# Two-block network on one core: the two rotary embeddings get their swapped halves from transfers inside SBUF instead of from permutation products

## The reference

```python
def apply_partial_rope(t, cos, sin):        # block one, ROPE_DIM = 16
    half = ROPE_DIM // 2
    t1 = t[..., :half]
    t2 = t[..., half:ROPE_DIM]
    rot = jnp.concatenate([t1 * c - t2 * s, t2 * c + t1 * s], axis=-1)
    return jnp.concatenate([rot, t[..., ROPE_DIM:]], axis=-1)

def _rope(x, pos):                          # block two, d = 64
    half = d // 2
    x1, x2 = xf[..., :half], xf[..., half:]
    out = jnp.concatenate([x1 * cos - x2 * sin, x2 * cos + x1 * sin], axis=-1)
```

## Time and profile before

| | |
|---|---|
| median of 3 runs | 1817.74 us (1811.52 to 1818.07) |
| the profiled execution | 1816.34 us, of which the trace's span is 1814.5 us |
| PE busy | 1708.3 us, 94% |
| DVE busy | 1047.8 us, 58% |
| ACT busy | 737.9 us, 41% |
| POOL busy | 63.0 us, 3% |
| chain that ended last | PE 81%, DVE 11%, ACT 5% |
| mean granted TensorE clock | 0.976 |

### The profile page before, as it was taken

The page is one execution under the profiler, slowest core; times in us unless marked ns, Lnnn a source line. Parts: engine busy times, 40 slices in busy tenths (PEclk is TensorE's granted clock), DMA queues, the critical chain, the costliest instruction groups (busy, mean ns, idle before and its releaser), DMA issues.

```text
span 1814.5 us, 22668 instructions
## 1 busy us (share of the span) xinstructions
PE 1708.3 (94%) x7488; PEld 1324.0 (73%) x7488; DVE 1047.8 (58%) x2091; ACT 737.9 (41%) x1392; POOL 63.0 (3%) x43
## 2 busy tenths in 40 slices
PE   5999999999998997799899999998999899999999
PEld 3777667777876765337688888886888678888887
DVE  7787766666456698963655564366444543333334
ACT  4363766663343233783443322324223244332322
POOL 0020000000000063000000000000000000000000
PEclk9999999999998997999899999998999899999999
DMA  6342334433331121002255554252333232232333
GB/s 232 135 166 95 123 133 158 145 139 134 95 91 57 47 61 45 1 1 70 73 198 193 185 186 163 91 199 83 102 97 100 70 93 92 93 102 95 97 101 104
DMA packets 55812, 201.65 MB, mean 111 GB/s; under 512 B 6192, under 2 KB 6320, under 8 KB 55600
## 3 DMA queue, kind: packets, MB, share of 16 engines
q1 hardware_dynamic: 55728, 200.57, 33.1%
HBM read 198.44 MB, written 2.10 MB: 111 GB/s over the span
## 4 chain that ended last, share of the span: by engine, by line
PE 81%; DVE 11%; ACT 5%; issue 2%; POOL 0%; DMA 0%; DVEq 0%; ACTq 0%; POOLq 0%
PE bank L450 25%; PE bank L452 24%; PE bank L451 24%; PE bank L563 2%; DVE G L1390 1%; ACT SB L964 1%; DVE SB L1535 1%; PE bank L552 1%; DVE H_lo L1384 1%; DVE W_lo L1320 1%; ACT PT L978 1%; PE bank L533 1%; DVE SB L1892 1%; PE bank L660 1%; DVE WORK L1810 1%
## 5 line engine op out<-in xcount | busy, mean ns | idle before, releaser
L450 PE MATMUL bank<-H_hi,W_hi 128*128 128x512 f32 x1416 | 578.7, 409 | 22.0 <-DVE H_lo L1384 12.2
L451 PE MATMUL bank<-H_lo,W_hi 128*128 128x512 f32 x1416 | 556.8, 393 | 0.0
L452 PE MATMUL bank<-H_hi,W_lo 128*128 128x512 f32 x1416 | 556.5, 393 | 0.0
L1320 DVE TENSOR_TENSOR W_lo<-RAW,W_hi 128x512 fp32r<-128x512 f32 x538 | 351.4, 692 | 196.3 <-ACT W_hi L839 180.6
L839 ACT CAST W_hi<-RAW 128x512 fp32r<-128x512 f32 x538 | 313.0, 618 | 234.9 <-PE bank L452 211.6
L450 PEld LDWEIGHTS bank<-H_hi,W_hi 128*128 128x128 f32 x1416 | 268.1, 189 | 120.0 <-issue 44.3
L451 PEld LDWEIGHTS bank<-H_lo,W_hi 128*128 128x128 f32 x1416 | 269.2, 190 | 58.1 <-issue 7.0
L452 PEld LDWEIGHTS bank<-H_hi,W_lo 128*128 128x128 f32 x1416 | 268.7, 190 | 58.0
L450 PE MATMUL bank<-A_hi,W_hi 128*128 128x512 f32 x352 | 137.0, 389 | 0.0
L452 PE MATMUL bank<-A_hi,W_lo 128*128 128x512 f32 x352 | 136.9, 389 | 0.0
L451 PE MATMUL bank<-A_lo,W_hi 128*128 128x512 f32 x352 | 136.9, 389 | 0.0
(11 more groups left out here) (255 smaller groups left out, 1915.9 us busy)
## 6 DMA issues: line engine op xcount, KB each, us to landing
RAW<-weights SPq DMA_DIRECT2D x269, 512.0 KB, 3.6
AW<-ada SPq DMA_DIRECT2D x100, 512.0 KB, 3.6
X<-x_t SPq DMA_DIRECT2D x4, 512.0 KB, 5.6
y_t<-X SPq DMA_DIRECT2D x8, 256.0 KB, 2.0
LW<-lru_w SPq DMA_DIRECT2D x1, 1024.0 KB, 12.9
CROW<-crow SPq DMA_DIRECT2D x1, 512.0 KB, 10.9
ROPE<-rope SPq DMA_DIRECT2D x1, 512.0 KB, 13.7
CS<-constants SPq DMA_DIRECT2D x1, 386.5 KB, 8.1
```

Of the source, the lines that this page charges most:

```text
L450: pe.matmul(dst, wh, ch(hi, k), start=(k == 0), stop=False)
L451: pe.matmul(dst, wh, ch(lo, k), start=False, stop=False)
L452: mm = pe.matmul(dst, wl, ch(hi, k), start=False, stop=(k == chunks - 1))
L1320: dve.tensor_tensor(W_lo[:, w], RAW[:, c:c + HALF], W_hi[:, w], ALU.subtract).then_inc(lo_done, 1)
```

## The change

The 24 products with a permutation (10 with rot1, 14 with rot2) are removed from PE. In their place SP issues, per chunk, four DMA transfers from SBUF to SBUF (`swap_halves`): for each of the two heads the lower half's rows go to where the upper half's belong and the other way round. In block one each moves 8 partitions of 512 columns (16 KB), in block two 32 partitions (64 KB). They write QX1 (block one, two buffers in the place of Y2) or QX (block two, two buffers), and DVE's second product reads that in place of the PSUM bank. In block one the rows that do not turn are set to zero once, by POOL, at the start. DVE waits for half_in, one semaphore for each buffer, 64 for the four transfers.

```diff
@@ block.sync @@
+            def swap_halves(c, dst, src, half):
+                for head in (0, HD):
+                    for a, b in ((head, head + half), (head + half, head)):
+                        sp.dma_start(dst[a:a + half, :], src[b:b + half, :]).then_inc(half_in[c % 2], 16)
+
+            def swap1(c):
+                sp.wait_ge(qraw, c + 1)
+                if c == 0:
+                    sp.wait_ge(x1_zero, 1)
+                if c >= 2:
+                    sp.wait_ge(rope_done, c - 1)
+                swap_halves(c, ch(QX1, c % 2), ch(QR1, c % 2), 8)
+
+            def swap2(i):
+                sp.wait_ge(head_in, i + 1)
+                sp.wait_ge(rope_done, 10 + i - 1)
+                swap_halves(i, ch(QX, i % 2), ch(QN, i % 3), 32)
+
             for t in range(0, T_FFN0):
                 raw(Tile(t + 4))
+                if T_Q < t <= T_Q + 10:
+                    swap1(t - T_Q - 1)
+                if T_QKV2 + 1 < t <= T_QKV2 + 7:
+                    swap2(t - T_QKV2 - 2)
+                if T_QKV2 + 9 < t <= T_QKV2 + 17:
+                    swap2(t - T_QKV2 - 4)
                 if t in ADA_AT:
                     ada_load(ADA_AT[t] % 4, ADA_AT[t] + 4)
@@ block.tensor @@
-            def rot1(c):
-                pe.wait_ge(qraw, c + 1)
-                if c >= 2:
-                    pe.wait_ge(rope_done, c - 1)
-                pe.matmul(ps[5 + c % 2][:], cs("rot1"), ch(QR1, c % 2), start=True, stop=True).then_inc(rot_mm, 1)
-
             for c in range(1, 10):
-                linear(Tile(T_Q + c), H_hi, H_lo, between=lambda k: rot1(c - 1) if k == 3 else None)
-            values(Tile(T_V), between=lambda k: rot1(9) if k == 3 else None)
+                linear(Tile(T_Q + c), H_hi, H_lo)
+            values(Tile(T_V))
-            def rot2(i):
-                pe.wait_ge(head_in, i + 1)
-                pe.wait_ge(rope_done, 10 + i)
-                bank = 5 if i == 13 else 3
-                pe.matmul(ps[bank][:], cs("rot2"), ch(QN, i % 3), start=True, stop=True).then_inc(rot_mm, 1)
...
+            pe.wait_ge(rope_done, 10 + 10)
             qk(16, (0, 1))
             query_columns(7)
-            rot2(13)
-            pe.wait_ge(rope_done, 10 + 13)
             qk(16, (2, 3))
             qk(17, (0, 1, 2))
...
-            pe.wait_ge(rope_done, 10 + 14)
             for s in range(16, 32):
+                if s < 18:
+                    pe.wait_ge(rope_done, (10 + 12, 10 + 14)[s - 16])
@@ block.gpsimd @@
+            pool.memset(QX1[:, :], 0.0).then_inc(x1_zero, 1)
@@ block.vector @@
             def rope1_out(c):
-                dve.wait_ge(rot_mm, c + 1)
+                dve.wait_ge(half_in[c % 2], 64 * (c // 2 + 1))
...
-                link(dve.tensor_tensor(RAB1[:, S:2 * S], ps[5 + c % 2][:], ROPE[:, S:2 * S], ALU.mult))
+                link(dve.tensor_tensor(RAB1[:, S:2 * S], ch(QX1, c % 2), ROPE[:, S:2 * S], ALU.mult))
...
             def rope2_out(i):
-                dve.wait_ge(rot_mm, 10 + i + 1)
+                dve.wait_ge(half_in[i % 2], 64 * (5 + i // 2 + 1))
...
-                turned(i, ch(QN, i % 3) if i < 6 else None, ps[5 if i == 13 else 3][:], dst)
+                turned(i, ch(QN, i % 3) if i < 6 else None, ch(QX, i % 2), dst)
...
-            rope2_out(13)
             score(16, 2)
             score(16, 3)
             minus_max(16)
+            rope2_out(13)
             for h in range(3):
                 score(17, h)
```

More of the change, by code:

```diff
@@ L37 @@
 _at = 0
-for _name, _n in (("ident", P), ("rot1", P), ("rot2", P), ("centre", P), ("sel_all", 1), ("sel_head", 2),
+for _name, _n in (("ident", P), ("rot2", P), ("centre", P), ("sel_all", 1), ("sel_head", 2),
                   ("mask_prev", P), ("mask_diag", P), ("sin_sign", 1), ("inv_freq", 1)):
@@ L62, in constant_columns @@
     put("ident", np.eye(P))
[L63 to L68, removed]
+    rot = np.zeros((P, P), np.float32)
+    for head in (0, HD):
+        for i in range(HD):
+            rot[head + (i + HD // 2) % HD, head + i] = 1.0
+    put("rot2", rot)
     put("sel_all", np.full((P, 1), 1.0 / (KC * P)))
@@ L280, in build @@
         QN = at("QN", 3 * S, unit[4] + S * 12)
+        QX = at("QX", 2 * S, unit[4] + S * 24)
         RAB = at("RAB", 2 * S, unit[6])
@@ L288, in build @@
         G1 = at("G1", 2 * S)
+        y2 = cursor[0]
         Y2 = at("Y2", 2 * S)
+        QX1 = at("QX1", 2 * S, y2)
         qr1 = sb1
@@ L320, in build @@
         ta_done, iu_done, states_done = sem("ta_done"), sem("iu_done"), sem("states_done")
-        qraw, rot_mm, rope_done, v_done = sem("qraw"), sem("rot_mm"), sem("rope_done"), sem("v_done")
+        qraw, rope_done, v_done = sem("qraw"), sem("rope_done"), sem("v_done")
+        x1_zero, half_in = sem("x1_zero"), [sem("half_in0"), sem("half_in1")]
         head_in, head_sq = sem("head_in"), sem("head_sq")
@@ L698, in in_qi1 @@
                     head_columns(ch(SQ, 0), 0, 4).then_inc(kcol_mm, 1)
-                if k == 3:
-                    rot2(0)
             def in_qi2(k):
@@ L704, in in_qi2 @@
                     head_rows(0)
-                if k == 3:
-                    rot2(1)
             def in_qi3(k):
@@ L711, in in_qi3 @@
                     pe.matmul(ps[7][:], cs("rot2"), ch(QR, 1), start=True, stop=True).then_inc(ki_rot, 1)
[L712 to L717, removed]
             def in_k1(k):
@@ L723, in in_k1 @@
                     head_columns(ch(SQ, 0), 8, 4).then_inc(kcol_mm, 1)
-                if k == 3:
-                    rot2(4)
                 if k < 7:
@@ L735, in in_values @@
                     head_rows(1)
-                if k == 3:
-                    rot2(5)
                 index(2, k)
@@ L747, in body @@
                             query_columns(c - 1)
-                        if k == 3:
-                            rot2(6 + c - 1)
                 return body
@@ L761, in _ @@
             linear(Tile(T_QKV2), H_hi, H_lo, first=h_ready(1))
-            for c, body in enumerate((in_qi0, in_qi1, in_qi2, in_qi3, in_k0, in_k1)):
+            for c, body in enumerate((in_qi0, in_qi1, in_qi2, in_qi3, None, in_k1)):
                 linear(Tile(T_QKV2 + 1 + c), H_hi, H_lo, between=body)
```

## The result

The changed kernel takes 1839.97 us (median of 4, 1836.04 to 1842.36) where the kernel before takes 1816.74 (median of 4, 1811.52 to 1818.07). The ratio is 1.0127, 95% interval 1.0105 to 1.0149: less than 2%, but clear of no change. The profiled execution of after took 1839.14 us with a span of 1837.4. The forecast was 1832, range 1815 to 1843, slower at 75%. The direction and the mechanism of block one held; the loss is 23 us where 15.5 were forecast.

A forecast was written before the change was run, and what follows sets the result against it. The prediction took PE to set the pace before the change, and a loop through SP's queue after it in block one. Block one +19.4, clock +1, block two -4.9 gave +15.5 on 1816.3: 1832 us, range 1815 to 1843.

The forecast's parts named there:

- The loop: Block one, chunks 1 to 7: transfers queue behind a load awaiting DVE's reduction; period 9.4 us, values 19.4 us later.
- The landing of 5.1 us: Block one: the four transfers land behind load and weight tile, 5.1 us after the reduction, 1.3 us of it covered.
- the lower bound: Block one: small transfers need not wait for large ones, landing after 2.9 us; period 7.2 us, values 4 us later.
- the upper one: Block one: each issue costs SP 0.43 us and the last lands in 4.5; landing 7.1 us, period 11.4 us.
- PE sets the pace, a period of 6.35: Block one before the change: DVE's turns come 6.35 us apart, each after waiting 0.8 us for PE's product.
- Rival A: Whole kernel: PE is the bound and transfers are hidden; up to 21 us gained on rotations, about 1801 us; 6%.
- The clock: Block one: PE's clock dips after idling, hidden inside the loop, costing 1 us (0 to 2) at the values' start.
- Rival C: Block one's loop: PE's clock falls and stays low, seven tiles cost 1.5 us more each, 1842 us; 12%.
- The 19 us pass to the end: After block one's values: everything behind needs them, so the 19 us delay carries through to the kernel's end.
- Block two: Keys gain 4.4 us, sine products lose 1, the moved last turn gains 1.5: together -4.9 us (-1 to -12).
- I take 1 us in all (0 to 3): Block two: eight sine products reading SBUF instead of PSUM beside GpSimd, 0 to 0.38 us more each, 1 us together.
- Rival B: Small transfers pass the large ones, landing in 2.9 us; block one loses 4, block two gains 5, 1816 us; 18%.

The follow-up runs named there:

- the four kernels of the table above: The changed kernel (1839.97 us) and three edits of it: two transfers per chunk in block one (1837.03), modulation loads cut to 16 partitions (1836.39), both edits (1829.85).
- block1_only: Changed kernel with block two's products and the last turn's old place restored, so only block one's rotations go by transfers: 1842.07 us, ratio 1.0134.
- the small load: Changed kernel with the modulation loads of steps 8 to 15 cut from 128 partitions to 16, all waits and issues kept: 1836.39 us.

## Why the prediction was right, and where its sizes were off

**The loop** was as forecast: SP's order, the four transfers behind load and tile, seven waits of DVE for a DMA, turns 9.8 to 10.2 us apart up to chunk 6 (9 to 10 was the mark), PE idle inside. The waits are longer than the mark of 3 to 4 us: 4.3 to 4.6, and 6.0 for chunk 7. Reversing the order alone takes all of it away, 29 us against the changed kernel.

**The landing of 5.1 us** was the mis-sized term. The six waits of the loop ended 5.6 to 5.85 us after the reduction (139.93 - 134.36 = 5.57; 150.06 - 144.21 = 5.85), and chunk 7's 7.2 us (171.75 - 164.55). The sum took SP's four issues for hidden behind the landing of the tile; they take 2.67 us and end 3.6 us after the reduction, and the transfers need some 2 us more: 147.81 to 150.06 is 2.25 us, 137.94 to 139.93 is 1.99. The value "2.0 us" stood in the lower bound and "each issue costs SP like a tile's" in the upper one; the truth joins the two, with 0.66 us in place of 0.43. Chunk 7 is the one behind whose transfers a weight tile is issued at once, at 168.21 above; in each of the four kernels of the table above it waits 1.4 to 1.6 us longer than the chunk before (6.00 against 4.64 us in the changed kernel). What holds it was not tried.

In numbers, +25.8 against +19.4: 0.7 us was lost before the first period, six periods of 10.0 in place of 9.4 are 3.7 us, chunk 7's landing 2.1.

**"PE sets the pace, a period of 6.35"** was read from two turns, and it holds for the whole stretch, though the earlier turns look otherwise. Here are turns of DVE, and then PE's rotations, in the trace of before:

```profile
110.65 0.69 DVE L1462 TENSOR_TENSOR RAB<-QR,ROPE 128x512 f32<-128x512 f32 x1
...
116.06 0.69 DVE L1462 TENSOR_TENSOR RAB<-QR,ROPE 128x512 f32<-128x512 f32 x1
```

```profile
107.62 1.02 PE L517 MATMUL bank<-QR,CS 128*128 128x512 f32 x2
...
113.97 1.02 PE L517 MATMUL bank<-QR,CS 128*128 128x512 f32 x2
...
120.31 1.02 PE L517 MATMUL bank<-QR,CS 128*128 128x512 f32 x2
```

The turns from 105.17 to 121.45 are 5.4 to 5.5 us apart with no wait before them, but the rotations are 6.35 us apart, and PE is busy for all of the 17.00 us from 105 to 122. DVE was behind (its instructions at 97 to 102 us took up to 1.77 us) and caught up; from 127.72 on it waits for PE at each turn. With the order reversed, PE still never waits from 106 to 144 and its tiles are 5.5 us apart. Up to the values seven rotations of 0.88 go, 6.2 us. Of these 0.8 are lost ahead, where PE waits for the late DVE (its first tile starts at 105.56, in before at 104.80), and 0.9 at the values (a wait of 2.38 us, in before 1.49); 4.5 remain, 150.98 to 146.48. Rival A's 21 us were out of reach: DVE needs 5.4 us for a chunk in either kernel, about as much as PE then needs for a tile.

**The clock**: +1 was forecast at the values. The windows of after (us, busy PE, PEld, DVE, ACT, POOL, PEclk, DMA, GB/s) show the dip of the earlier trace rows many times, here in one period of the loop and at the values:

```profile
132.00:134.00 2.00, 0.00 (x0) 0.00 (x0) 1.67 (x3) 0.96 (x2) 0.00 (x0) 1.00 0.00 0
134.00:136.00 2.00, 0.89 (x2) 0.82 (x3) 1.57 (x4) 1.83 (x4) 0.00 (x0) 0.59 0.33 49
136.00:138.00 2.00, 2.00 (x6) 1.52 (x6) 0.00 (x0) 0.79 (x2) 0.00 (x0) 0.50 0.96 379
138.00:140.00 2.00, 2.00 (x7) 1.52 (x6) 0.07 (x1) 0.00 (x0) 0.00 (x0) 0.50 0.35 133
140.00:142.00 2.00, 2.00 (x8) 1.59 (x7) 1.92 (x3) 0.00 (x0) 0.00 (x0) 0.70 0.00 0
142.00:144.00 2.00, 1.69 (x8) 1.04 (x6) 1.72 (x2) 0.90 (x2) 0.00 (x0) 1.00 0.00 0
...
178.00:180.00 2.00, 2.00 (x11) 2.00 (x11) 1.93 (x3) 0.00 (x0) 0.00 (x0) 0.50 0.54 202
```

Half speed is 1.2 GHz. In the loop a slow tile is hidden, as forecast: the one above ends at 143.7, and PE then still waits 1.46 us for the next split. Rival C's lasting half clock did not come: the clock is back at 1.00 by 142. The shift grows by 0.9 us from the values' splits to the first attention step. What the forecast lacked is that the dips of before, which it had read, need not recur: at 170 to 180 before was granted 0.83 on average, and after at the same work, 195 to 205, 1.00. From the last attention step of block one to the last norm, before (first row) and after (second):

```profile
397.00:569.00 172.00, 160.76 (x689) 128.48 (x688) 95.48 (x167) 66.63 (x119) 0.00 (x0) 0.95 0.31 100
```

```profile
422.00:592.50 170.50, 157.58 (x690) 125.67 (x689) 95.60 (x168) 66.71 (x120) 0.00 (x0) 0.98 0.30 100
```

The same 690 matmuls take 3.2 us less at the higher clock, and the stretch is 1.5 us shorter: in this execution part of the loss came back. It is this execution's luck and not the change: the same stretch takes 172.0 to 172.2 us in all eleven other traces, and in block1_only the loss passes on whole (+27.1, +27.0). "The 19 us pass to the end" was right, and the 3.3 us that came back here made the forecast's error look smaller than it was.

**Block two** came out at -1.2 (+23.4 to +22.2) where -4.9 stood, and its sign, an interval 3 to 5 us shorter up to the end of the queries, did not come: 140.9 us before (569.1 to 710.0), 141.4 after (592.5 to 733.9). The part where PE sets the pace gave 4.5 us, as forecast (4.4), and the moved turn 1.7 (1.5). The step that failed is "I take 1 us in all (0 to 3)" for the sine product's operand in SBUF beside GpSimd: the queries' part lost 5.0 to 5.1. It counted the eight products alone; over block two the traces have 1.5 us more for the products, 2.0 for DVE's splits (23.1 for 21.1), 1.1 for the sums on line 1744 and 1.4 of waiting for a transfer of the queries, 6.0 in all, of which DVE's other idle time takes up a part. Why the splits and sums are slower stays open. The longest product took 1778 ns, not the 1070 of the earlier trace rows from which the bound came. The waits for transfers were small, as forecast: 2.5 us in two of 14 chunks.

**Rival B** (small transfers pass the large, 2.9 us) was refuted by the 5.6 us, and the small load shows what it left out: with the load in front cut to an eighth, the transfers land 1.35 us after SP's last issue, but SP alone needs 3.6 us to get there. The fixed cost of 2.0 us that the Trainium skill gives (DMA: Bandwidth & Descriptors, "Anatomy of one DMA — SWDGE (gpsimd) path"), and that the prediction cites, is for transfers issued by GpSimd. These are issued by SP; the last of the four, with the small load, takes 2.0 us from the start of its issue (144.60 to 146.61). The Trainium skill (DMA: Bandwidth & Descriptors, "Queues, rings and completion order") has each DMA engine take one ring's descriptors in order. The 3.25 us after SP's last issue with the full load, where the small load has 2.0, agree. By that rule alone four transfers and two would have given the same period; the measured 10.02 and 9.64 differ.

The sum with the measured terms: +26.7 at the first attention step, -3.3 on the way to block two, -4.5 + 5.0 - 1.7 there, +0.7 behind: +22.9, the difference of the spans. The forecast's +15.5 was short by 7.4: 6.4 in block one up to the values, 3.7 in block two and 0.6 in the rest, less the 3.3 that came back.

## What to carry to other kernels

Before a transfer is put into the queue of an in-order issuer, look at what the entry in front of it waits for; if that is work of the engine which will wait for the new transfer, the queue closes a loop, and each round of it costs the full latency, here 10 us in place of the 5.5 with the order reversed. The cure is the order, not a faster transfer: shrinking what stood in front brought 0.7 us a period, standing ahead of it 4.5. And count an issuer's time for many small transfers as you would count an engine's: four of 16 KB held SP for 2.7 us, six times what a 512 KB tile takes.

## What the runs showed of the hardware that was not expected

- SP takes 0.66 us to issue a transfer of 8 partitions within SBUF (2.67 us for 4, 1.32 for 2) and 0.60 us for one of 32 partitions (2.41 us for 4), against 0.33 to 0.58 us for a 512 KB load from HBM.
- DVE's products and sums with both operands in SBUF take 0.69 us, but now and then 1.0 to 1.8 us where GpSimd works; the same product from PSUM never took more than 0.694 in any of the traces. The longest case of the changed kernel, in the timeline of DVE and then of POOL (GpSimd):

```profile
700.48 1.78 DVE L1739 TENSOR_TENSOR RAB<-QX,ROPE 128x512 f32<-128x512 f32 x1
```

```profile
699.97 1.74 POOL L1287 TENSOR_TENSOR QR<-QN,ROPE 128x512 f32<-128x512 f32 x1
```

DVE's product began inside GpSimd's, and ended 0.55 us after it (702.26 against 701.71). The Trainium skill (SBUF — State Buffer, "Who interferes with whom") says that a DVE instruction with two SBUF inputs contends with a GpSimd instruction that reads SBUF, and that one with at most one, outside the two-port modes, does not. The traces agree: the eight products of before, which read one operand from PSUM, took 0.68 to 0.69 us, also at 652.63 and 678.85, inside instructions of GpSimd.
- In a loop of 10 us with PE idle for some 3 us of it, the granted clock went to 0.50 and back to 1.00 within a period; no lasting level set in.
